# Gate and up products of a feed-forward layer as seven block products instead of eight

## The reference, cut to what matters

```python
def conv_ffn(h, prev, w_gate, w_up, conv_w, conv_b, w_down):   # D_MODEL 1024, D_FF 2816
    g = h @ w_gate
    u = h @ w_up
    gp = jnp.concatenate([prev.astype(g.dtype), g], axis=1)
    gc = conv_b
    for i in range(CONV_W):                                     # 3
        gc = gc + conv_w[i] * gp[:, i:i + l]
    y = (jax.nn.gelu(gc) * u) @ w_down
    return y, gp[:, -(CONV_W - 1):]
# hp = hp + conv_ffn(rms_norm(hp, norm_ffn[l]), ...)
```

## Time and profile before

| | |
|---|---|
| median of 3 runs | 1596.8 us (1596.42 to 1599.4) |
| the profiled execution | 1597.14 us, its span 1595.6 us |
| PE busy | 1571.7 us, 99% |
| DVE busy | 783.5 us, 49% |
| ACT busy | 565.6 us, 35% |
| POOL busy | 387.9 us, 24% |
| mean granted clock of PE | 0.996 of full speed |

### The profile page before, as it was taken

How to read it: one execution, slowest core, us unless ns; L and a number is a source line. 1 busy time by engine, 2 the same in 40 slices (tenths; PEclk the granted TensorE clock), 3 DMA queues, 4 the chain that set the end, 5 groups by cost and what they waited for, 6 DMA issues and landing times.

```text
span 1595.6 us, 27497 instructions
## 1 busy us (share of the span) xinstructions
PE 1571.7 (99%) x10810; PEld 1497.5 (94%) x10810; DVE 783.5 (49%) x1022; ACT 565.6 (35%) x888; POOL 387.9 (24%) x421
## 2 busy tenths in 40 slices
PE   9999989999999999999999999999999999999998
PEld 6899879999999999999988997799999999999997
DVE  3324786665543245553322248857554522555522
ACT  4332266245552123322222323643455411333312
POOL 3370020432221012222306402115222200221223
PEclk9999999999999999999999999999999999999998
DMA  5321253222322223322233213612233232232222
GB/s 199 123 76 54 93 186 140 77 99 96 129 97 92 86 90 109 105 67 77 71 102 123 86 47 135 231 59 72 94 130 105 86 102 89 94 129 79 65 73 92
DMA packets 44415, 161.99 MB, mean 102 GB/s; under 512 B 5793, under 2 KB 8257, under 8 KB 43265
## 3 DMA queue, kind: packets, MB, share of 16 engines
q1 hardware_dynamic: 39680, 129.70, 25.0%
q0 software_dynamic: 2464, 28.26, 4.4%
q10 hardware_dynamic: 2208, 3.15, 0.5%
HBM read 149.08 MB, written 30.88 MB: 113 GB/s over the span
## 4 chain that ended last, share of the span: by engine, by line
PE 89%; DVE 6%; ACT 2%; issue 2%; POOL 1%; POOLq 0%; DVEq 0%; ACTq 0%
PE PSUM L1490 62%; PE PSUM L1540 13%; PE PSUM L1565 6%; PE PSUM L1466 4%; PE PSUM L1780 1%; DVE RS L987 1%; PE PSUM L1718 1%; PE PSUM L1556 0%; PE PSUM L1713 0%; DVE SM L1195 0%; ACT WH L728 0%; ACT PS L799 0%; POOL YT L691 0%; DVE XNL L1357 0%; DVE CT L1392 0%
## 5 line engine op out<-in xcount | busy, mean ns | idle before, releaser
L982 DVE TENSOR_TENSOR WL<-RAW,WH 128x1024 fp32r<-128x1024 f32 (+1 forms) x216 | 294.4, 1364 | 489.1 <-ACT WH L728 488.6
L728 ACT ACTIVATE WH<-RAW 128x1024 fp32r<-128x1024 f32 (+1 forms) x216 | 211.9, 982 | 553.9 <-PE PSUM L1490 385.9
L1490 PE MATMUL PSUM<-XFH,WH 128*128 128x320 f32 x1056 | 240.9, 310 | 1.8 <-DVE WL L982 1.2
L1490 PE MATMUL PSUM<-XFH,WL 128*128 128x320 f32 x1056 | 240.0, 309 | 0.0
L1490 PE MATMUL PSUM<-XFL,WH 128*128 128x320 f32 x1056 | 240.0, 309 | 0.0
L1490 PE MATMUL PSUM<-XNH,WH 128*128 128x320 f32 x864 | 198.2, 310 | 1.0 <-DVE XNL L1357 1.0
L1490 PE MATMUL PSUM<-XNL,WH 128*128 128x320 f32 x864 | 196.8, 309 | 0.0
L1490 PE MATMUL PSUM<-XNH,WL 128*128 128x320 f32 x864 | 196.7, 309 | 0.0
L1490 PEld LDWEIGHTS PSUM<-XFH,WH 128*128 128x128 f32 x1056 | 176.2, 188 | 3.0 <-issue 2.7
L1490 PEld LDWEIGHTS PSUM<-XFL,WH 128*128 128x128 f32 x1056 | 176.3, 188 | 0.0
L1490 PEld LDWEIGHTS PSUM<-XFH,WL 128*128 128x128 f32 x1056 | 176.2, 188 | 0.0
(11 more groups left out here) (230 smaller groups left out, 2341.5 us busy)
## 6 DMA issues: line engine op xcount, KB each, us to landing
RAW<-w_gu SPq DMA_DIRECT2D x88, 512.0 KB, 3.5
RAW<-w_in SPq DMA_DIRECT2D x40, 512.0 KB, 3.6
RAW<-w_down SPq DMA_DIRECT2D x32, 384.0 KB, 3.0
RAW<-w_down SPq DMA_DIRECT2D x32, 320.0 KB, 2.7
CAK<-ca_kt SPq DMA_DIRECT2D x16, 512.0 KB, 4.6
CAV<-ca_v SPq DMA_DIRECT2D x16, 512.0 KB, 5.1
RAW<-w_out SPq DMA_DIRECT2D x16, 512.0 KB, 3.6
ca_kt_copy<-ca_kt POOLq DMA_DIRECT2D x16, 512.0 KB, 4.9
```

The costliest lines, as they stand in the source:

```text
L728: nc.scalar.activation(WH[:, s, 0:width], RAW[:, s, 0:width], ACT.Copy).then_inc(hi_ready[s], 1)
L982: nc.vector.tensor_tensor(WL[:, s, 0:width], RAW[:, s, 0:width], WH[:, s, 0:width].bitcast(F32), ALU.subtract).then_inc(lo_ready[s], 1)
L1490: last = nc.tensor.matmul(PSUM[:, b + a, 0:HALF], w[:, s, P * k:P * (k + 1)], x[:, HALF * a:HALF * (a + 1)], start=start and k == 0 and w ...
```

## The change

Of the 22 gate and up tiles of a layer the first 3 (`PLAIN`) stay as they were. For the other 19 the two products of a tile are taken as one product of a 2x2 block matrix, [up; gate] (rows) by two halves of the width (`a11 a12; a21 a22`, each 4 width tiles x 128 features), with the 2x2 block matrix of the frames (`b11` ..., halves of the width by halves of the frames). Strassen's scheme (in Winograd's form) needs seven block products: `a11 b11`, `s2 t2`, `s1 t1`, `s3 t3`, `a12 b21`, `a22 t4`, `s4 b22`, where `s1` to `s4` are sums and differences of weight blocks and `t1` to `t4` of frame blocks. Each is 4 x 3 matmuls on 320 columns.

DVE makes the sums of weight blocks for each tile (`block_sum`), ACT rounds all seven (`block_round`), DVE takes seven remainders (`block_rest`). The frame blocks are made once a layer, during the plain tiles: DVE scales the frames by gain and norm factor (`scale_frames`), takes four differences (`frame_sum`) and, after ACT's rounding, seven remainders (`frame_rest`). The seven results lie in seven PSUM banks and are added up as they are moved out: ACT copies the first into `RS`, DVE makes the running sums (`take_second`, `take_third`, `take_gate_second`, `take_up_first`, `take_gate_first`, `take_up_second`). A second buffer `RAW2` holds the weights of every other tile. The multiplication of gelu and up moves from POOL to DVE (`multiply`). The loops over the tiles on SP, ACT, DVE and PE are unrolled, and convolution, gelu and y of a tile are done during the next tile. Lines without a + or - are unchanged.

```diff
+PLAIN = 3
+DOWN_UNIT = FFN_UNIT + 2 * PLAIN
+UNITS = DOWN_UNIT + 2 * KT * FFN_HALVES
 SLOT_USES = UNITS // 2
+QUARTER = KT // 2 * P
+PRODUCTS = ("a11", "s2", "s1", "s3", "a12", "a22", "s4")
+MOVING = {"a11": "b11", "s2": "t2", "s1": "t1", "s3": "t3", "a12": "b21", "a22": "t4", "s4": "b22"}
+BLOCK_SUMS = ("s1", "s2", "s3", "s4")
+FRAME_PARTS = ("b11", "t1", "t2", "t3", "b21", "t4", "b22")
+FOLDED = FF_TILES - PLAIN
...
+        BLOCK_BANK = {"a11": 0, "s2": 1, "s1": 2, "s3": 3, "a12": 4, "a22": 7, "s4": 6}
...
+                def load_quarters(t):
+                    if t == PLAIN:
+                        column_sums.wait(sp, l, "ffn")
+                    elif t == PLAIN + 1 or t == FF_HALF + 1:
+                        n = (FFN_UNIT, PLAIN - 1) if t == PLAIN + 1 else (DOWN_UNIT, KT - 1)
                         for j in range(2):
-                            load_unit(l, FFN_UNIT + j, w_gu[l, h, f, j], extra=h * FFN_EXTRA + f)
-                    with sp.Fori(0, KT) as m:
+                            sp.wait_ge(lo_ready[j], CREDIT + unit_use(l, *n) + 1)
+                    else:
+                        sp.wait_ge(block_lo, block_count(l, t - 2, "a22"))
+                    for j in range(2):
+                        sp.dma_start(raw_of(t)[:, j, :], w_gu[l, t // FF_HALF, t % FF_HALF, j])\
+                            .then_inc(quarters_loaded[t % 2], 16)
...
-                    pool.wait_ge(y_lo, CREDIT + n)
-                    pool.wait_ge(up_copied, CREDIT + n + 1)
-                    pool.wait_ge(gelu_done, n + 1)
-                    nc.gpsimd.tensor_tensor(prompt_of(YT[:, :]), prompt_of(UT[:, :]),
-                                            halves(CT[:, 0:SEQ]), ALU.mult).then_inc(product_done, 1)
...
+                def block_round(t, name):
+                    if name[0] == "a":
+                        act.wait_ge(quarters_loaded[t % 2], quarters_count(l, t))
+                    else:
+                        act.wait_ge(sum_done, sum_count(l, t, name))
+                    if t in (PLAIN, FF_HALF) and PRODUCTS.index(name) < 4:
+                        n = (FFN_UNIT, PLAIN - 1) if t == PLAIN else (DOWN_UNIT, KT - 1)
+                        product_wait(act, l, n[0] + PRODUCTS.index(name) // 2, n[1])
+                    elif folded_index(l, t):
+                        act.wait_ge(block_used, block_count(l, t, name) - len(PRODUCTS))
+                    nc.scalar.activation(block_slot(name)[0], block_source(t, name), ACT.Copy).then_inc(block_hi, 1)
...
+                def y_round(t):
+                    if t == FF_HALF:
+                        product_wait(act, l, DOWN_UNIT + 1, KT - 1)
+                    act.wait_ge(product_done, CREDIT + 2 * (l * FF_TILES + t) + 2)
+                    nc.scalar.activation(YH[:, t % FF_HALF, :], YT[:, :], ACT.Copy).then_inc(y_hi, 1)
...
+                    for t in range(FF_HALF if h else PLAIN + 1, FF_HALF * (h + 1)):
+                        last, inner = t == FF_HALF * (h + 1) - 1, t != FF_HALF
+                        block_round(t, "s4")
+                        take_first(t)
+                        if not last:
+                            block_round(t + 1, "a11")
+                        if inner:
+                            gelu(t - 1)
+                        if last:
+                            down_round(0, h, 0)
+                        else:
+                            block_round(t + 1, "s2")
+                        if inner:
+                            y_round(t - 1)
+                        if last:
+                            down_round(1, h, 0)
+                        else:
+                            block_round(t + 1, "s1")
+                            block_round(t + 1, "s3")
+                        if not last:
+                            block_round(t + 1, "a12")
+                            block_round(t + 1, "a22")
+                        tap(t)
...
+                def block_sum(t, name):
+                    a = {"s1": ("a21", "a22", ALU.add), "s2": ("s1", "a11", ALU.subtract),
+                         "s3": ("a11", "a21", ALU.subtract), "s4": ("a12", "s2", ALU.subtract)}[name]
+                    dve.wait_ge(quarters_loaded[t % 2], quarters_count(l, t))
+                    if name in ("s2", "s4"):
+                        dve.wait_ge(sum_done, sum_count(l, t, name) - (1 if name == "s2" else 2))
+                    used = {"s1": (t - 1, "s3"), "s2": (t - 1, "s4"), "s3": (t, "s1"), "s4": (t, "s2")}[name]
+                    if folded_index(l, used[0]) >= 0 and used[0] >= PLAIN:
+                        dve.wait_ge(block_lo, block_count(l, *used))
+                    nc.vector.tensor_tensor(block_source(t, name), block_source(t, a[0]), block_source(t, a[1]), a[2])\
+                        .then_inc(sum_done, 1)
+                def block_rest(t, name):
+                    dve.wait_ge(block_hi, block_count(l, t, name))
+                    high, low = block_slot(name)
+                    nc.vector.tensor_tensor(low, block_source(t, name), high.bitcast(F32), ALU.subtract)\
+                        .then_inc(block_lo, 1)
+                def scale_frames(k):
+                    nc.vector.scalar_tensor_tensor(out=XN[:, k, :], in0=X[:, k, :],
+                                                   scalar=GAIN[:, bass.ds(l, 1), 1, k], in1=RS[:, :],
+                                                   op0=ALU.mult, op1=ALU.mult).then_inc(frame_step, 1)
...
+                def multiply(t):
+                    n = l * FF_TILES + t
+                    dve.wait_ge(y_lo, CREDIT + n)
+                    dve.wait_ge(up_copied, CREDIT + n + 1)
+                    dve.wait_ge(gelu_done, n + 1)
+                    nc.vector.tensor_tensor(prompt_of(YT[:, :]), prompt_of(UT[:, :]),
+                                            halves(CT[:, 0:SEQ]), ALU.mult).then_inc(product_done, 1)
...
+                def take_second(t):
+                    i = folded_index(l, t)
+                    dve.wait_ge(block_used, block_count(l, t, "s2"))
+                    dve.wait_ge(first_taken, i + 1)
+                    dve.wait_ge(up_copied, CREDIT + l * FF_TILES + t)
+                    nc.vector.tensor_tensor(RS[:, HALF:], block_bank("s2"), RS[:, 0:HALF], ALU.add).then_inc(folded, 1)
+                def take_third(t):
+                    i = folded_index(l, t)
+                    dve.wait_ge(block_used, block_count(l, t, "s3"))
+                    dve.wait_ge(gate_copied, CREDIT + 2 * (l * FF_TILES + t))
+                    dve.wait_ge(folded, 4 * i + 1)
+                    nc.vector.tensor_tensor(U3[:, :], block_bank("s3"), RS[:, HALF:], ALU.add).then_inc(folded, 1)
+                def take_gate_second(t):
+                    gate_free(t)
+                    dve.wait_ge(folded, 4 * folded_index(l, t) + 2)
+                    nc.vector.tensor_tensor(streams[:, 1, :, 2:], streams_of(block_bank("s1")[:, 0:HALF_SAMPLE]),
+                                            streams_of(U3[:, 0:HALF_SAMPLE]), ALU.add)
+                    nc.vector.tensor_tensor(GP[:, 2 + HALF_PROMPT:CONV_ROW], block_bank("s1")[:, HALF_SAMPLE:],
+                                            U3[:, HALF_SAMPLE:], ALU.add).then_inc(gate_copied, 1)
+                    nc.vector.tensor_tensor(RS[:, HALF:], block_bank("s1"), RS[:, HALF:], ALU.add).then_inc(folded, 1)
+                def take_up_first(t):
+                    dve.wait_ge(block_used, block_count(l, t, "a12"))
+                    dve.wait_ge(product_done, CREDIT + 2 * (l * FF_TILES + t))
+                    nc.vector.tensor_tensor(UT[:, 0:HALF], block_bank("a12"), RS[:, 0:HALF], ALU.add).then_inc(folded, 1)
+                def take_gate_first(t):
+                    dve.wait_ge(block_used, block_count(l, t, "a22"))
+                    nc.vector.tensor_tensor(streams[:, 0, :, 2:], streams_of(block_bank("a22")[:, HALF_PROMPT:]),
+                                            streams_of(U3[:, HALF_PROMPT:]), ALU.add)
+                    nc.vector.tensor_tensor(GP[:, 2:2 + HALF_PROMPT], block_bank("a22")[:, 0:HALF_PROMPT],
+                                            U3[:, 0:HALF_PROMPT], ALU.add).then_inc(gate_copied, 1)
+                def take_up_second(t):
+                    dve.wait_ge(block_used, block_count(l, t, "s4"))
+                    dve.wait_ge(folded, 4 * folded_index(l, t) + 3)
+                    nc.vector.tensor_tensor(UT[:, HALF:], block_bank("s4"), RS[:, HALF:], ALU.add)\
+                        .then_inc(up_copied, 1)
...
+                    for t in range(FF_HALF if h else PLAIN + 1, FF_HALF * (h + 1)):
+                        last, inner = t == FF_HALF * (h + 1) - 1, t != FF_HALF
+                        if inner:
+                            take_up_second(t - 1)
+                            convolve(t - 1)
+                        block_rest(t, "s4")
+                        if not last:
+                            block_sum(t + 1, "s1")
```

(106 more changed lines are left out.)

296 lines of the change are left out of this document (224 added, 72 removed).

## The result

The changed kernel takes 1635.27 us (median of 4 runs, 1634.48 to 1636.45) against 1597.13 us before: a ratio of 1.0238, 95% interval 1.0226 to 1.0250. The forecast was 1636 us, slower. The profiled execution took 1634.68 us, its span 1633.1 us, 37.5 us more than before.

What follows compares the result with a forecast made beforehand. PE bounded the kernel before; DVE, at 14.95 us a folded tile against PE's 14.1, would bound it after. Start +9.3, halves +5.3 and +3.6, down phases +1.4: +19.6 a layer, +39 on 1597.1, 1636 us (1612 to 1668).

Steps and rivals of the forecast that it cites:

- Products: PE, folded tiles: 84 matmuls instead of 96, 12.3 us against 14.1, 67 us less if nothing else ends later.
- DVE passes and self-waits: DVE, each folded tile: 12.9 us of passes at start-to-start pace plus 0.6 us of self-waits, within 14.95 us a tile.
- The three chained operations: DVE: s2 after s1, s3's sum after s1's remainder, first gate piece after U3, each waiting 0.19 us more.
- the last rival: DVE, folded tiles: every operation pays its full duration, 2.1 us more a tile, 17.0 in all, about 1698 us; chance 0.04.
- The stall: DVE, between multiply and s1's remainder: waits while ACT rounds y, then s1; 1.44 us a tile.
- The rest of the halves: From tile 4 and in the second half: 103.9 us against 98.6, +5.3, and 158.5 against 154.9, +3.6, per layer.
- The start: First gate row to tile 4: 52.8 us of DVE work behind its reciprocal; tile 4 at 68.1 instead of 58.8, +9.3.
- Down phases: Second part of each first down product waits about 1.7 us for the last tile's y; +1.4 for both halves.
- Sum: All delays together: +19.6 us a layer, +39 us on 1597.1, giving 1636 us.
- The low end of the range: Whole kernel: forecast range 1612 to 1668 us, given 0.76, from bounds, 1% on DVE, the clock and part of a rival.
- its own bounds: Whole kernel: +29 us with least hand-overs and self-waits, +67 with the loop's 0.14; 1% on DVE paces moves it 5.
- Clock: PE: half rate behind waits of 2 us, absorbed inside tiles; only the four ends of halves feel it, 0 to +8 us.

Runs made afterwards that it cites:

- experiment 2: Changed kernel with two moves on DVE, second and third takes put between chained operations so none directly follows the one it needs; 1625.96 us, ratio 1.0176.
- experiment 1: Changed kernel with ACT rounding s1 of the coming tile ahead of y of the tile before; 1596.08 us, ratio 0.9987.
- Experiments 7 and 8: 7: five plain tiles a layer instead of three, on experiment 6, 1563.89 us; 8: seven frame remainders cut to 64 elements, on the changed kernel, 1628.30 us.
- experiment 3: Changed kernel without the low-weight terms of block products a12, a22 and s4, 12 of 84 matmuls a folded tile; 1640.73 us, ratio 1.0262.
- experiment 6: Edits of experiment 1 and experiment 2 together, plus three more moves in DVE's order; 1569.25 us, ratio 0.9820.
- experiment 5: Experiment 1 with the product of gelu and up put back from DVE on POOL; 1607.46 us, ratio 1.0061.

## Why the prediction was right, step by step

- **Products**: 0.147 us a matmul, 12.3 us a folded tile, as said; nothing of the gain reached the steady tile.
- **DVE passes and self-waits**: the tile came out at 14.93 against 14.95. The three chained operations start 0.78, 0.80 and 0.61 after their predecessors where 0.60, 0.60 and 0.41 are the pace: 0.18, 0.20, 0.20, forecast 0.19 each. Paying each operation's full duration, the last rival, is excluded: rows of 0.68 still follow each other in 0.60. Its price of 17.0 us was itself too high: there are 25 operations to a tile, not 27, and six of them are followed by a gap anyway, so full durations make 16.5 us. (The Trainium skill's formula, in VectorE: DVE Perf Modes, "The TRN2 errata", gives the 0.69 that one row lasts; the trace agrees with it for the duration alone.) That the self-waits are on the path, and not hidden, experiment 2 shows: it took 0.41 us of them from each tile, and nearly that went from the time.
- **The stall**: 1.41 for 1.44, shown by experiment 1 to be the cause of the slowdown in size too: without it the kernel is level with before.
- **The rest of the halves**: tile 4 to the first down product took 498.13 - 394.62 = 103.5 us, forecast 103.9; tile 11 to the second down product 735.81 - 576.86 = 158.95, forecast 158.5. Tile by tile it holds as well: the first tiles took 12.4 and 13.05 us (12.3 and 13.2) and 12.3 three times and 13.9 (the same), the middle ones 14.95 in the mean; the last with its wait 18.4 and 18.3 (18.6 and 17.9), though the wait ahead of the first down product was 2.1 and not 4. The rows of PE that begin these stretches or end them:

```profile
394.62 0.38 PE L2240 MATMUL PSUM<-XNH,WH 128*128 128x320 f32 x1 [0.99 <-DVE WL L1559]
...
498.13 0.42 PE L1878 MATMUL PSUM<-YH,WH 128*128 128x320 f32 x1 [2.14 <-DVE UT L1662]
...
576.86 0.31 PE L2240 MATMUL PSUM<-XNH,WH 128*128 128x320 f32 x1
...
735.81 0.63 PE L1878 MATMUL PSUM<-YH,WH 128*128 128x320 f32 x1 [3.64 <-DVE UT L1662]
```

- **The start**: tile 4 began 394.62 - 327.19 = 67.4 us after the first gate row, forecast 68.1, so +8.6 for +9.3. The size was right; its reason was only half so. The prediction laid 52.8 us of DVE work end to end behind the reciprocal. In truth PE ends the last plain up product at 375.4 us, after a wait of 2.8 us of its own for a weight remainder (L1151 in the list of waits, once a layer), and DVE takes that product at 376.03, with less than a microsecond of delay; only the work behind that point is DVE's alone. Experiments 7 and 8 were forecast with the same series, and gave 5 of 18 and 7 to 8.5 of 17 us. In the changed kernel the two lines nearly meet, which is why the sum held; that was luck.
- **Down phases**: +1.4 a layer was said, for a wait of 1.7 us for the last tile's y. From the first to the last down product the halves took 78.6 and 78.8 us instead of 78.5 and 77.8, +1.1. The size is near, the reason was wrong: PE waited for y once, 0.9 us in the first phase, no longer than before; the longer phase is the second, whose head ran at a lower clock (below).
- **Sum**: 8.6 + 4.9 + 4.1 + 1.1 = 18.7 us in the first layer, forecast 19.6; the span grew by 37.5, forecast 39. The low end of the range, 1612, is not what its own bounds give (1597.1 + 29, less 5, is 1621); nothing hangs on it.
- **Clock**: half rate behind the waits came as said, and it cost nothing inside the tiles. A waiting tile after L1656's wait, by microsecond (PE busy, PEld, DVE, ACT, POOL, clock):

```profile
1438.00:1439.00 1.00, 1.00 (x6) 1.00 (x7) 1.00 (x2) 0.09 (x1) 0.00 (x0) 0.83 0.00 0
1439.00:1440.00 1.00, 1.00 (x6) 1.00 (x5) 1.00 (x3) 0.00 (x0) 0.00 (x0) 0.50 0.00 0
...
1442.00:1443.00 1.00, 1.00 (x8) 1.00 (x8) 1.00 (x2) 1.00 (x4) 0.69 (x3) 0.96 0.11 33
```

The lost microsecond is taken from the next wait for L1656, which is then about half as long. So PE's tiles often alternate between 16.06 and 13.79 us, and DVE's last 14.93 as ever. Such a shorter wait:

```profile
1423.01 0.42 PE L2240 MATMUL PSUM<-XNH,WH 128*128 128x320 f32 x1 [0.88 <-DVE RS L1656]
```

At the ends of the halves, where it could have cost up to 8 us, the first down phase of the first layer began at full clock and the second at 0.83 over its first ten microseconds, which lies in the +1.1 of the down phases:

```profile
735.00:745.00 10.00, 9.19 (x53) 9.20 (x54) 5.73 (x10) 3.27 (x4) 0.89 (x3) 0.83 0.17 54
```

## What to carry to other kernels

Before cutting work on the busy engine, add up what the cut puts on the next one in the same stretch by start-to-start times: here DVE's 7.3 us of 14.1 left some 5 to a tile of 12.3, and the change brought 5.6 in passes, 0.6 in chains and 1.4 in a stall. Then read the two queues side by side for a result that goes to another engine and back: an instruction of the other engine that stands between the two, however short, was paid in full on the path here, and moving one line past it was worth 39 us. A series of work laid end to end gives the right end only if one engine has it all; where two lines merely meet, taking from either one gives less than its size.

## What the runs showed of the hardware that was not expected

- Taking 12 matmuls out of each folded tile (experiment 3) left the time no shorter and by the ratios rather longer (1.0262 against 1.0238, with intervals that overlap a little). PE waited 4.4 us ahead of the first down phase instead of 2.1, and its granted clock then stood at 0.50 (1.2 GHz) for some 5 us where it had been 1.00 (2.4 GHz); the phase began as long after the first gate row as before and ended 1.6 us later. All four down phases of this run began at 0.50 (in the changed kernel three fell to it, for a shorter time), and they hold 5.3 of the 8.4 us. Idle PE time ahead of a stretch that PE bounds can have a price of its own. The price is not fixed: behind its wait of 2.8 us, the second down phase of experiment 6 took only 77.7 us.
- A DVE operation that meets a POOL product seems to stand still for it (experiment 5): the sum of 512 began 0.27 us after POOL's product of 1.33, and ended 0.55 after that product's end, 1.61 in all. The next DVE operation ran in 0.48 as ever, though POOL's second product was still under way, itself long for 128 elements (0.88). In both cases measured, a sum of 512 and a remainder of 1024, the price was 0.9 us, a little less than what was left of POOL's product (1.06 and 1.03). The Trainium skill (SBUF — State Buffer, "SBUF: two separate sides") has it that the two engines take a port pair in turns, for a whole instruction, when a DVE operation has two inputs in SBUF and the GpSimd one reads there; the 0.92 us lost agree with that roughly for the first product, and the short DVE operation behind it reads one input from PSUM. That this is the cause was not tried apart.
